# The second product of each filter tap over all 128 rows, with the low part of the weights formed for both row halves

## The reference, cut to what matters

```python
h = jnp.sin(fr1 * (z @ w1 + b1))
h = jnp.sin(fr2 * (h @ w2 + b2))
h = (h @ w3).reshape(L, 2, HY_ORDER, HY_WIDTH)      # h: (L, 64), w3: (64, 2048)
h = h * jnp.exp(-t * deltas)[:, None, None, :]
kern = jnp.concatenate([h[:, 0], zeros, h[:0:-1, 1]], axis=0)
kern = kern * rsqrt(sum(kern ** 2, axis=0))
return jnp.fft.rfft(kern, axis=0)
```

## Time and profile before

| | |
|---|---|
| median of 3 runs | 2400.17 us (2398.79 to 2403.77) |
| the profiled execution: its own time | 2402.85 us |
| the profiled execution: span from the first to the last instruction | 2401.1 us |
| TensorE busy with matmuls | 2275.6 us, 95% of the span, 10340 instructions |
| TensorE busy with weight loads (beside the matmuls) | 1859.8 us, 77% |
| VectorE busy | 1188.1 us, 49% |
| ScalarE busy | 785.5 us, 33% |
| GpSimd busy | 145.8 us, 6% |
| mean granted clock of TensorE | 0.982 |

### The profile page before, as it was taken

One profiled execution on the slowest core, in us unless ns is written; L12 is line 12 of the kernel. 1 busy time (PEld: TensorE's weight loads), 2 busy tenths in 40 slices (PEclk: granted clock), 3 DMA queues, 4 the chain that ended last, 5 costly groups with the idle time before them and its releaser, 6 DMA issues.

```text
span 2401.1 us, 26125 instructions
## 1 busy us (share of the span) xinstructions
PE 2275.6 (95%) x10340; PEld 1859.8 (77%) x10340; DVE 1188.1 (49%) x1655; ACT 785.5 (33%) x1193; POOL 145.8 (6%) x163
## 2 busy tenths in 40 slices
PE   6999999998998979877899999999999999999998
PEld 4778877887786767666688888888888887888886
DVE  6676676554832756656456333343333334324332
ACT  5432333245434434534344211221222122324221
POOL 0221122000111000100000000000000000000000
PEclk9999999999999999999999999999999999999999
DMA  4344444454655665856645111121111112535442
GB/s 142 110 140 132 121 130 145 130 168 134 190 174 166 201 192 151 244 154 184 212 132 176 49 62 53 62 79 53 57 53 62 62 53 90 180 116 173 155 149 84
DMA packets 213588, 307.23 MB, mean 128 GB/s; under 512 B 15480, under 2 KB 143864, under 8 KB 213466
## 3 DMA queue, kind: packets, MB, share of 16 engines
q1 hardware_dynamic: 200858, 256.00, 35.0%
q0 software_dynamic: 11312, 46.14, 5.3%
q10 hardware_dynamic: 1296, 3.41, 0.4%
HBM read 207.38 MB, written 72.16 MB: 116 GB/s over the span
## 4 chain that ended last, share of the span: by engine, by line
PE 51%; DVE 0%; ACT 0%; issue 0%; DVEq 0%; POOL 0%
PE mlp_acc L128 10%; PE mlp_acc L130 10%; PE mlp_acc L129 10%; PE mlp_dacc L128 7%; PE mlp_dacc L129 7%; PE mlp_dacc L130 7%; PE mlp_acc L2596 0%; DVE out_s_lo L2494 0%; DVE up_u L245 0%; ACT up_u L2437 0%; DVE mlp_h_lo L2516 0%; DVE out_w_lo L2489 0%; DVE down_d_lo L2538 0%; ACT out_s_hi L2412 0%; DVE up_u L249 0%
## 5 line engine op out<-in xcount | busy, mean ns | idle before, releaser
L128 PE MATMUL mlp_acc<-mlp_h_hi,up_w_hi 128*128 128x512 f32 x1056 | 411.1, 389 | 0.2 <-DVE mlp_h_lo L2516 0.2
L130 PE MATMUL mlp_acc<-mlp_h_hi,up_w_lo 128*128 128x512 f32 x1056 | 410.8, 389 | 0.0
L129 PE MATMUL mlp_acc<-mlp_h_lo,up_w_hi 128*128 128x512 f32 x1056 | 410.8, 389 | 0.0
L2521 DVE TENSOR_TENSOR up_w_lo<-up_w_raw,up_w_hi 128x1024 fp32r<-128x1024 f32 x44 | 53.8, 1225 | 388.2 <-ACT up_w_hi L2429 388.2
L128 PEld LDWEIGHTS mlp_acc<-mlp_h_hi,up_w_hi 128*128 128x128 f32 x1056 | 198.2, 188 | 41.6 <-DVE mlp_h_lo L2516 0.6
L130 PEld LDWEIGHTS mlp_acc<-mlp_h_hi,up_w_lo 128*128 128x128 f32 x1056 | 198.2, 188 | 41.2
L129 PEld LDWEIGHTS mlp_acc<-mlp_h_lo,up_w_hi 128*128 128x128 f32 x1056 | 198.2, 188 | 41.1
L128 PE MATMUL mlp_dacc<-down_d_hi,down_s_hi 128*128 128x512 f32 x528 | 206.8, 392 | 5.3 <-DVE down_d_lo L2538 5.3
L129 PE MATMUL mlp_dacc<-down_d_lo,down_s_hi 128*128 128x512 f32 x528 | 206.6, 391 | 0.0
L130 PE MATMUL mlp_dacc<-down_d_hi,down_s_lo 128*128 128x512 f32 x528 | 206.4, 391 | 0.0
L2429 ACT ACTIVATE up_w_hi<-up_w_raw 128x1024 fp32r<-128x1024 f32 x44 | 46.6, 1059 | 460.1 <-PE mlp_acc L130 460.1
(11 more groups left out here) (243 smaller groups left out, 3902.2 us busy)
## 6 DMA issues: line engine op xcount, KB each, us to landing
in_w_raw<-arg_w_in_t SPq DMA_DIRECT2D x58, 512.0 KB, 3.6
down_s_raw<-g_scratch SPq DMA_DIRECT2D x48, 512.0 KB, 4.4
up_w_raw<-arg_w_up_t SPq DMA_DIRECT2D x44, 512.0 KB, 3.5
g_scratch<-up_prod POOLq DMA_DIRECT2D x22, 768.0 KB, 3.5
filt_tab<-arg_fwd SPq DMA_DIRECT2D x32, 512.0 KB, 3.8
mix_classes<-mix_split SPq DMA_DIRECT2D x48, 256.0 KB, 8.5
mix_kf<-k_scratch SPq DMA_DIRECT2D x48, 256.0 KB, 2.8
mix_split<-mix_classes SPq DMA_DIRECT2D x48, 256.0 KB, 5.0
```

The source lines that it names most:

```text
L128: pe.matmul(out, w_hi, x_hi, start=first, stop=False)
L129: pe.matmul(out, w_hi, x_lo, start=False, stop=False)
L130: return pe.matmul(out, w_lo, x_hi, start=False, stop=last)
L2521: dve.tensor_tensor(w_lo[i % 2][:, :, :], raw[i % 2][:, :, :], w_hi[i % 2][:, :, :].bitcast(F32), ALU.subtract).then_inc(sem["w_low"], 1)
```

## The change

The second product of a tap takes all 128 rows of `h2` and of `w3_lo`, and `w3_lo` is formed for 128 rows. The second product then also adds low by low, which the 64-row form leaves out. The number of instructions and the number of columns stay as they are.

```diff
-            w3_hi, w3_lo = f.sb("w3_hi", [P, 2, 2, HC], F32R), f.sb("w3_lo", [HID, 2, 2, HC], F32R)
+            w3_hi, w3_lo = f.sb("w3_hi", [P, 2, 2, HC], F32R), f.sb("w3_lo", [P, 2, 2, HC], F32R)
...
                     pe.matmul(cbank[:, 0, :], h2[:, rows], wide[0], start=True, stop=False)
-                    pe.matmul(cbank[:, 0, :], h2[0:HID, rows], wide[1], start=False, stop=True).then_inc(sem["tapped"], 1)
+                    pe.matmul(cbank[:, 0, :], h2[:, rows], wide[1], start=False, stop=True).then_inc(sem["tapped"], 1)
...
                 def low_w3(o):
                     dve.wait_ge(sem["w3_high"], o + 1)
-                    dve.tensor_tensor(w3_lo[:, :, :, :].rearrange("p h x c -> p x h c"), flat[0:HID, 1, :].rearrange("p (x h c) -> p x h c", x=2, h=2),
-                                      w3_hi[0:HID, :, :, :].rearrange("p h x c -> p x h c").bitcast(F32), ALU.subtract).then_inc(sem["w3_low"], 1)
+                    dve.tensor_tensor(w3_lo[:, :, :, :].rearrange("p h x c -> p x h c"), flat[:, 1, :].rearrange("p (x h c) -> p x h c", x=2, h=2),
+                                      w3_hi[:, :, :, :].rearrange("p h x c -> p x h c").bitcast(F32), ALU.subtract).then_inc(sem["w3_low"], 1)
```

## The result

| | before | after |
|---|---|---|
| median of the runs | 2401.09 us (2396.91 to 2407.64, 6 runs) | 2384.88 us (2382.36 to 2393.07, 6 runs) |
| span of the profiled execution | 2401.1 us | 2380.5 us |
| TensorE busy | 2275.6 us | 2253.8 us |

The ratio is 0.9929, 95% interval 0.9914 to 0.9945: 17 us less (13 to 21); the two medians are 16.2 us apart. The forecast was 17.6 us less, 2382.6 us, with a range of 2376 to 2394.

The account below looks back on a forecast made before the run. The prediction took PE's instruction starts to bound the stretch with the taps. 19.0 us gained less 1.4 us lost to VectorE gave 17.6 us, so 2382.6 us from 2400.17, with a range of 2376 to 2394.

Parts of the forecast that it names:

- rival A: At the tap: rows are no cost, the late starts come from something else there; 2400.2 us, chance 0.07.
- The size, 19.0 us: Gain in PE's starts at 48 taps: 0.40 us each before a projection product, 0.39 us each before a transform.
- The three steps: Start-to-start times from L990 through L991 to the second product behind it; each to become about 0.23 us.
- The loss of 1.4 us in closed loops: At seven taps bound by VectorE's multiply, 0.2 us of each gain turns into a wait for VectorE.
- rival B: Between taps, waits for VectorE take back half the gain (2390.7 us), or only entry to 64 rows cost (2395.9); chance 0.09.
- Part 3 of the prediction: Work behind the tap on other engines, such as VectorE's staging: nothing put on it, a loss kept in the rivals.
- low_w3 and what follows: Subtraction over 128 rows costs nothing (0.02 us at most); the head start passes in full through gates and later stages.
- Rival C: Second stage's wait for mix_split, 17.9 us, grows and eats the gain, making the kernel slower; chance 0.04.

Follow-up runs that it names:

- The product alone: Kernel before with the second product over 128 rows, lower rows of the low part zero, subtraction still at 64 rows: 2384.13 us, ratio 0.9939.
- 64 rows twice: Kernel before with the tap's first product over 64 rows too, so both take 64: 2403.26 us, ratio 1.0006.
- one pair of changes against two: Kernel before, each tap product cut into two of 256 columns: order 128, 64, 64, 128 rows 2401.25 us; order 128, 64, 128, 64 rows 2422.27 us.

## Why the prediction was right

**The place and the cause.** TensorE's starts set the time of this stretch, and 17 us taken off them came off the whole. The late weight loads of L991, of L128 and, behind taps, of L1012 were one effect: a change between products over 128 rows and products over 64. The product alone, 64 rows twice, and one pair of changes against two show this; rival A, a cost at the tap that has nothing to do with rows, is out. The Trainium skill's rule in TensorEngine Tiling (Array Packing), Tiling Modes, that a change of tiling mode (of how the array's rows and columns are divided) drains TensorE, was on the right side: 96 rows beside 128 were free, 64 and 32 were not. That the price is such a drain is not shown, since the profile names no mode. The Trainium skill's columns rule (TensorE: Matmul & The Clock Gate, LDWEIGHTS), which spoke for rival A, holds for the load's duration, 183 ns at 64 rows and 190 ns at 128, and a product over 96 rows lasts as long as one over 128. It is silent on when the load can start, and the gain lay there.

**The size, 19.0 us.** The three steps fell as forecast, from 0.32, 0.43 and 0.33 us to 0.23, 0.23 and 0.24. 48 x 0.39 to 0.40 us is right. The prediction told the 0.40 us as a cost paid on both sides of the 64-row product; the finer reading is that each change costs 0.1 us on either side of the first product of the new kind.

**The loss of 1.4 us in closed loops.** Seven taps were counted, and the same seven wait, each with 0.2 us of its gain lost. After the change the two taps of the earlier trace rows read:

```profile
297.20 0.39 PE L990 MATMUL in_cbank<-filt_w_hi,filt_h_parts 128*128 128x512 f32 x1
...
298.61 0.50 PE L990 MATMUL in_cbank<-filt_w_hi,filt_h_parts 128*128 128x512 f32 x1
```

1.41 us where 1.40 was forecast and 1.60 was before.

**What was missing.** From first to last tap it gained 16.2 us. The sum of 17.6 is for 48 taps, and between the first and the last lie 47 gains, so 17.2 was due there and some 1.0 us is missing. Both executions start the same products in the same order in this stretch, so the loss can be found by laying them side by side. It lies in small waits, mostly of the kind that rival B describes. Part 3 of the prediction put nothing on VectorE's other work, and here it costs a little:

- Two groups of transposes wait longer for VectorE's copy, 0.5 us in all (the row L966 <- L1195 above). The larger one, first as it is now and then as it was before:

```profile
312.98 0.33 PE L966 MATMUL in_tbank<-all_ident,in_u 128*128 128x128 f32 x1 [0.52 <-DVE in_u L1195]
```

```profile
324.35 0.66 PE L966 MATMUL in_tbank<-all_ident,in_u 128*128 128x128 f32 x4 [0.15 <-DVE in_u L1195]
```

- An eighth tap, at 201.36 us, waits 0.1 us for VectorE's multiply, too short for the rows of waits.
- Two transforms behind taps start late and take 0.2 us each of their taps' gain, 0.4 us in all:

```profile
202.02 0.73 PEld L1012 LDWEIGHTS in_cbank<-filt_cr,filt_tab 128*128 128x128 f32 x4 [0.36 <-issue]
...
358.49 0.73 PEld L1012 LDWEIGHTS in_cbank<-filt_cr,filt_tab 128*128 128x128 f32 x4 [0.38 <-issue]
```

The "issue" of the second hides a transfer. Before a transform TensorE waits for its table (issued at line 800) and for a copied result (line 1007); this wait and the issue of the table:

```profile
L1007 PEldq EVENT_SEMAPHORE  x1: 839/839/839, 357.6 to 357.6; - x1
```

```profile
352.36 0.37 SPq L800 DMA_DIRECT2D filt_tab<-arg_fwd  x1
```

This table takes 6.1 us to land (352.36 to 358.4), the wait ends at 357.6 + 0.84 = 358.5, and the load follows at 358.49. The first, at 202.02, starts 0.1 us behind the end of VectorE's copy of a result (L1325, 201.22 to 201.90), which fits the other wait; that this copy held it is not shown.

The agreement of 17.6 forecast with 17 measured is closer than the account of it: the interval (13 to 21) can't tell 17.6 from 16.6, which is what is left with this loss.

**low_w3 and what follows.** The subtraction went from 1214 to 1222 ns for double the rows, and made alone it changed nothing that can be measured. The long wait at the gates kept its length (7.88 us, 7.74 before) and came 17.0 us earlier, so nothing of the head start was lost there. Rival C did not happen: the wait for mix_split is the same.

## What to carry to other kernels

A small product between large ones is not free because it has few rows: where its neighbours use 128 rows and it uses 64 or 32, the pair of changes costs about 0.40 us here (float32r, full clock), nearly twice the 0.23 us of a whole 512-column product. Fill the rows (with zeros, or with a term that helps), or put such products next to each other; 96 rows were as good as 128. To find it, count from start to start, since a TensorE that read 100% busy hid 19 us here, and look for weight loads that are late for "issue". First rule out a wait of TensorE's own queue, which hides behind the same word.

## What was not expected of the hardware

- A change between 128 and 64 rows costs 0.20 us, half ahead of the first product of the new kind and half behind it, with 256 columns as with 512. A pair of changes with 32 rows costs the same 0.40 us in the end-to-end time; 96 rows beside 128 cost nothing.
- A weight load of 128 columns lasts 0.19 us, but two of them take 0.29 us: four products of 256 columns instead of two of 512 cost no time that can be measured (ratio 0.9996).
